# A transformer block on one core: the conditioning vector taken up ahead of the other parameters, and two GpSimd operations of the second norm moved to VectorE

## The reference, cut to what matters

```python
mod_x = jax.nn.silu(c) @ lp['ada_w'] + lp['ada_b']
mod_c = jax.nn.silu(c_ctx) @ lp['ada_w'] + lp['ada_b']
shx1, scx1, gx1, shx2, scx2, gx2 = [t[:, None, :] for t in jnp.split(mod_x, 6, axis=-1)]
hx = modulate(rms_norm(x, lp['norm_pre_mix']), shx1, scx1)
hc = modulate(rms_norm(ctx, lp['norm_pre_mix']), shc1, scc1)
...
x = x + gx1 * rms_norm(merge_branches(px[..., MIX_IN:], yx_a, yx_b, lp), lp['norm_post_mix'])
hx = modulate(rms_norm(x, lp['norm_pre_ffn']), shx2, scx2)
x = x + gx2 * rms_norm(swiglu(hx, lp), lp['norm_post_ffn'])
```

## Time and profile before

| | us |
|---|---|
| median of 3 runs | 2158.22 |
| lowest and highest run | 2155.16, 2163.36 |
| the profiled execution, its own time | 2160.06 |
| its span in the trace | 2158.2 |
| TensorE busy | 2024.2 |
| VectorE busy | 1252.0 |
| ScalarE busy | 808.1 |
| GpSimd busy | 269.8 |

### The profile page before, as it was taken

The page is one execution under the profiler, slowest core; times in us unless marked ns, Lnnn a source line. Parts: engine busy times, 40 slices in busy tenths (PEclk is TensorE's granted clock), DMA queues, the critical chain, the costliest instruction groups (busy, mean ns, idle before and its releaser), DMA issues. The chain is left out here.

```text
span 2158.2 us, 35947 instructions
## 1 busy us (share of the span) xinstructions
PE 2024.2 (94%) x15475; PEld 1655.1 (77%) x15475; DVE 1252.0 (58%) x1160; ACT 808.1 (37%) x895; POOL 269.8 (12%) x132
## 2 busy tenths in 40 slices
PE   5899999999999989977899899989999999999998
PEld 3367888888788876656788688878888888888886
DVE  2365666665556347768878487564445455444445
ACT  2232121212263235435544465533334333433333
POOL 0023121312304034301000020120000000000000
PEclk9899999999999999989999999999999999999999
DMA  8988888887555389978442578626556555555553
GB/s 301 382 288 310 314 313 320 290 319 269 153 147 131 88 230 313 283 164 194 97 91 58 93 233 321 215 78 195 185 184 194 188 185 191 194 204 192 192 193 116
DMA packets 355505, 453.62 MB, mean 210 GB/s; under 512 B 106062, under 2 KB 261054, under 8 KB 338094
## 3 DMA queue, kind: packets, MB, share of 16 engines
q1 hardware_dynamic: 347760, 440.59, 64.4%
q10 hardware_dynamic: 7614, 11.10, 1.4%
HBM read 413.43 MB, written 38.22 MB: 209 GB/s over the span
## 5 line engine op out<-in xcount | busy, mean ns | idle before, releaser
L221 DVE TENSOR_TENSOR f_w_lo<-t_w_raw,f_w_hi 128x2048 fp32r<-128x2048 f32 x130 | 297.9, 2292 | 363.5 <-ACT f_w_hi L214 363.5
L214 ACT ACTIVATE f_w_hi<-t_w_raw 128x2048 fp32r<-128x2048 f32 x132 | 252.7, 1916 | 436.7 <-PE pf L2963 288.6
L2961 PE MATMUL pf<-f_w_hi,h 128*128 128x512 f32 x688 | 268.5, 390 | 0.0
L2963 PE MATMUL pf<-f_w_hi,h 128*128 128x512 f32 x688 | 267.7, 389 | 0.0
L2962 PE MATMUL pf<-f_w_lo,h 128*128 128x512 f32 x688 | 267.7, 389 | 0.0
L214 ACT ACTIVATE p_w_hi<-h_w_raw 128x2048 fp32r<-128x2048 f32 x48 | 89.2, 1909 | 334.0 <-DVE stage L761 252.2
L906 DVE SCALAR_TENSOR_TENSOR late_acc<-h_of_x,siluc,late_acc 128x2048 f32<-128x2048 f32 x60 | 162.7, 2712 | 44.7 <-DMA h_of_x<-in_ada_w 43.1
L3009 PE MATMUL d_out<-f_w_hi,hid 128*128 128x512 f32 x704 | 176.4, 390 | 0.3 <-DVE f_w_lo L221 0.3
L266 PE MATMUL p_in<-h,p_w_lo 128*128 128x512 f32 x448 | 174.3, 389 | 0.0
L265 PE MATMUL p_in<-h,p_w_hi 128*128 128x512 f32 x448 | 174.3, 389 | 0.0
L264 PE MATMUL p_in<-h,p_w_hi 128*128 128x512 f32 x448 | 174.3, 389 | 0.0
(11 more groups left out here) (429 smaller groups left out, 3470.3 us busy)
## 6 DMA issues: line engine op xcount, KB each, us to landing
h_of_x<-in_ada_w SPq DMA_DIRECT2D x64, 1024.0 KB, 5.2
h_w_raw<-in_w_in SPq DMA_DIRECT2D x48, 1024.0 KB, 7.6
t_w_raw<-in_ffn_w_gate SPq DMA_DIRECT2D x44, 1024.0 KB, 5.2
t_w_raw<-in_ffn_w_up SPq DMA_DIRECT2D x44, 1024.0 KB, 5.2
t_w_raw<-in_ffn_w_down SPq DMA_DIRECT2D x44, 1024.0 KB, 4.9
h_w_raw<-in_ada_w SPq DMA_DIRECT2D x32, 1024.0 KB, 10.5
gate_w<-in_w_in SPq DMA_DIRECT2D x30, 1024.0 KB, 6.0
t_w_raw<-in_w_out SPq DMA_DIRECT2D x16, 1024.0 KB, 5.8
```

The costliest lines, as they stand in the source:

```text
L214: act.activation(self.hi[:, m % self.S, 0:w] if to is None else to, self.raw[:, s, 0:w], ACT.Copy)\
L221: eng.tensor_tensor(lo, self.raw[:, s, 0:w], b32(hi), ALU.subtract)\
L2961: pe.matmul(o, h[:, 0], hi[:, at], start=k == 0, stop=False)
L2963: return pe.matmul(o, h[:, 1], hi[:, at], start=False, stop=k == KT - 1)
```

## The change

In the first stage, `c` and `c_ctx` are the only rows that ScalarE loads. The other 22 transfers go to SyncE behind the fourth modulation tile. TensorE transposes c by itself, VectorE copies it to a tile of its own (`ccol`), ScalarE's sigmoid stands between the first and the second square, and the two silu operations stand ahead of the statistics on VectorE. The products of the first modulation tile come ahead of the first pair of turns, one pair now follows each of the first eight tiles, and the three transposes of the parameters stand behind the fourth pair. At the second norm, the low part of weight tile 3 and the copy of the first half's h leave GpSimd; VectorE makes the low part directly behind the second diagonal, and the copy behind the last low part of h.

```diff
-                for tile, row, n, w, src in pieces:
-                    act.dma_start(prow[row:row + n, tile, 0:w], src).then_inc(s_prow, 16)
-                for n in range(4):
+                for tile, row, n, w, src in c_pieces:
+                    act.dma_start(prow[row:row + n, tile, 0:w], src).then_inc(s_crow, 16)
...
+                token_square(0)
+                act.wait_ge(s_ccol, 1)
+                act.activation(sigc[:], ccol[:], ACT.Sigmoid).then_inc(s_sig, 1)
+                for n in range(1, 4):
+                    token_square(n)
...
+                    if t == RAW - 1:
+                        sp.wait_ge(s_const, 1)
+                        for tile, row, n, w, piece in other_pieces:
+                            sp.dma_start(prow[row:row + n, tile, 0:w], piece).then_inc(s_prow, 16)
...
-                    if t < 7:
-                        for b in range(2 + 2 * t, 4 + 2 * t):
+                    if t == 0:
+                        pe.wait_ge(s_diag, 4)
+                    if t < 8:
+                        for b in range(2 * t, 2 * t + 2):
                             turn(b)
+                    if t == 3:
+                        pe.wait_ge(s_const, 10)
+                        pe.wait_ge(s_prow, 16 * len(other_pieces))
...
-                pool.wait_ge(fring.lo_odd, 1)
-                fring.split_lo(pool, 3, 3, to=[t[:] for t in apart[3]])
-                pool.wait_ge(s_hlo0, 4)
-                pool.wait_ge(s_o, 8)
-                pool.tensor_copy(h2[:, :, :, 0:P].rearrange("p a k t -> p (a k) t"),
-                                 b32(h0).rearrange("p a k t -> p (a k) t")).then_inc(s_h0, 1)
...
                 unit_rows(1)
+                dve.wait_ge(fring.lo_odd, 1)
+                fring.split_lo(dve, 3, 3, to=[t[:] for t in apart[3]])
                 for g in range(4):
                     h_of(1, g)
                     if g:
                         h_lo(g - 1)
                 h_lo(3)
+                dve.wait_ge(s_o, 8)
+                dve.tensor_copy(h2[:, :, :, 0:P].rearrange("p a k t -> p (a k) t"),
+                                b32(h0).rearrange("p a k t -> p (a k) t")).then_inc(s_h0, 1)
```

More of the change, by code:

```diff
@@ L335, in phase_inputs @@
     s_const = sem("i_constants_made")
+    s_crow, s_cT, s_ccol = (sem(f"i_c_{n}") for n in ("rows_landed", "transposed", "columns_copied"))
     s_prow = sem("i_param_rows_landed")
@@ L376, in phase_inputs @@
         sigc = alloc(st, "sigc", [P, 2 * KT])
+        ccol = alloc(st, "c_columns", [P, 2 * KT])
+        C_ROW = COL["c"] % P
+        c_rows = prow[C_ROW:C_ROW + 2 * KT, COL["c"] // P, :]
+        c_pieces = [p for p in pieces if p[0] == COL["c"] // P and C_ROW <= p[1] < C_ROW + 2 * KT]
+        other_pieces = [p for p in pieces if not (p[0] == COL["c"] // P and C_ROW <= p[1] < C_ROW + 2 * KT)]
         sel = alloc(st, "sel", [P, 2])
@@ L485, in columns @@
                     last.then_inc(s_modp, 1)
[L486 to L494, removed]
+                pe.wait_ge(s_crow, 16 * len(c_pieces))
+                pe.transpose(p_col[:, 0:2 * KT], c_rows, ident[C_ROW:C_ROW + 2 * KT, C_ROW:C_ROW + 2 * KT]).then_inc(s_cT, 1)
                 pe.wait_ge(s_sc, 1)
@@ L502, in _ @@
                     last.then_inc(s_used, 1)
-                    if t < 7:
-                        for b in range(2 + 2 * t, 4 + 2 * t):
+                    if t == 0:
+                        pe.wait_ge(s_diag, 4)
+                    if t < 8:
+                        for b in range(2 * t, 2 * t + 2):
                             turn(b)
+                    if t == 3:
+                        pe.wait_ge(s_const, 10)
+                        pe.wait_ge(s_prow, 16 * len(other_pieces))
+                        for r in range(PROWS):
+                            last = pe.transpose(p_col[:, r * P:(r + 1) * P], prow[:, r, :], ident[:])
+                        last.then_inc(s_prmT, 1)
                     if q == 1 and p:
@@ L517, in _, with token_square @@
                 act.wait_ge(s_const, 1)
[L518 to L520 removed]
+                for tile, row, n, w, src in c_pieces:
+                    act.dma_start(prow[row:row + n, tile, 0:w], src).then_inc(s_crow, 16)
+                def token_square(n):
                     act.wait_ge(s_xt[n], 16)
@@ L562, in _ @@
                     dve.tensor_scalar(diag[:, n, :], ident[:], stat[:, 1, n:n + 1], None, ALU.mult).then_inc(s_diag, 1)
+                for b in range(8):
+                    evac(b)
+                dve.wait_ge(s_prmT, 1)
+                dve.tensor_copy(prm[:], p_col[:, 0:PROWS * P]).then_inc(s_prm, 1)
                 dve.wait_ge(s_prm, 1)
[L564 to L571 removed]
                 mu = prm[:, COL["mu"]:COL["mu"] + 29]
@@ L613, in _ @@
                 row(0)
-                for b in range(10, 14):
+                for b in range(8, 12):
                     evac(b)
@@ L618, in _ @@
                     if j == 0:
-                        evac(14)
-                        evac(15)
+                        for b in range(12, 16):
+                            evac(b)
                     row(2 * j + 1)
```

17 lines of the change are left out of this document (8 added, 9 removed).

## The result

The changed kernel took 2146.08 us (median of 7 runs, 2141.4 to 2148.42) beside 2160.73 us for the kernel before (7 runs): a ratio of 0.9921, with a 95% interval of 0.9905 to 0.9937. (The ratio on record is not the quotient of the two medians, which is 0.9932 and lies in the same interval.) The forecast was 2145.3, in a range of 2141 to 2150. A second comparison gave 2146.1 beside 2161.74 and again 0.9921 (0.9900 to 0.9942). The time came out 0.8 us from the forecast, and part of that is luck. The forecast had a gain of 12.9 us, a ratio of 0.9940, which lies just outside the first interval and at the edge of the second. The measured gain is larger: some 17 us by the ratio (13.6 to 20.5), 14.7 by the medians. The times agree this closely because the seven runs of the kernel before have a median 2.5 us above the 2158.22 that the forecast started from.

The account below looks back on a forecast made before the run. TensorE, busy 94% of the span, was taken as the bound; the norm's 9.1 us plus the first stage's 3.8 (4.2 - 0.9 + 0.5) gave 12.9, from 2158.22 to 2145.3 us, range 2141 to 2150.

Parts of the forecast that it names:

- The norm, 9.1 us: Second norm: without GpSimd's two operations beside VectorE's additions, TensorE saves 7.0 us of idle time and 2.1 of slow clock.
- The copy: Second norm: VectorE's copy of 128x4096 takes at most 4.6 us, hidden at cost 0 with 0.7 us slack.
- Rival (e): Second norm: VectorE's copy is far dearer than a subtraction and makes the kernel slower, 2166.8 us; 2%.
- The low part of tile 3: Second norm: on VectorE directly behind the diagonal, 2.29 us, hidden with 1.6 us to spare.
- The fourth square: First stage, ScalarE: starts at 14.2 instead of 18.38, with turns 4.68 us behind it, 4.2 us earlier.
- The clock of the first pair: First stage, TensorE: working on the first tile just before shortens the slow part by 0 to 1.7 us, taken as 0.5.
- The transposes: First stage, TensorE: three parameter transposes now stand between turns instead of inside the wait, costing 0.9 us.
- (d): First stage: c lands late, at 16.9, so only 5.3 us are gained, 2152.9 us; 3%.
- SyncE's 22 issues: First stage: the parameter transfers moved to SyncE end by 12 to 19 us, hidden.
- Handed on to the stage's end: First stage: its 3.8 us gain reaches the stage's end, because the transfers behind 48.44 are the same and start earlier.
- Rival (a): First stage: its gain is lost before the stage ends, with a second half-clock stretch costing 3.6 us; 2148.9 us; 15%.
- Rival (b): First stage: the half-clock stretch near its end goes, adding 3.6 us for 16.5 in all, 2141.7 us; 8%.

Follow-up runs that it names:

- e12: The changed kernel without any further change, traced a third time and timed again; traced span 2146.4 us.
- e1: Against the kernel before, only the first stage's part of the change, GpSimd keeping its two operations at the norm; 2153.08 us, ratio 0.9968.
- e10: Against the changed kernel, TensorE turns the first two token tiles ahead of the first modulation product again; traced span 2147.4 us.
- e8: Against the changed kernel, the 22 other parameter transfers are issued by ScalarE again, right behind c; traced span 2145.8 us.

## Why the prediction was right, and where it was not

- **The norm, 9.1 us:** 6.97 of idle time (t0 to t1: 21.81 to 14.84, the same in every trace that has this part) and 2.09 of clock, 9.06. The additions were priced at 1.18 + 3 x 0.7 = 3.3 and took 3.17. Only the instruction beside the first was misnamed: it is the product for h, no low part.
- **The copy:** taken at its upper bound of 4.6, measured 2.28. The step that failed is the row that stood for it: 4096 columns of the copy take as long as 2048 of the subtraction. And the reading that the trace has no copy of VectorE from SBUF to SBUF was wrong. It has several, these two among them (count, busy us, mean ns):

```profile
L1486 DVE COPY first_b<-ident 64x512 f32<-64x512 f32 x2 | 0.8, 418 | 0.0
L1487 DVE CAST eye_r<-ident 128x128 fp32r<-128x128 f32 x1 | 0.2, 227 | 0.0
```

  By these two rows a further column costs 0.5 ns, and 4096 columns some 2.2 us, an estimate that would have been right to 0.1. The Trainium skill, "VectorE: DVE Perf Modes", section "Mode 2×_2P — use both read ports for one tensor", says that an operation with one SBUF tensor can make two results per cycle, in float32 too, and one with two tensors can't. By that the price is halved as well, and the 2.28 us of both agree. The copy's cost was 0 either way, and the slack at this place is more than was given. Rival (e) had no ground.
- **The low part of tile 3:** 2.28, directly behind the diagonal, hidden, as said.
- **The fourth square** started at 13.29 and not 14.2: the landing of the last tokens was taken from before (11.9 us after issue), and it came 0.9 sooner. The 4.68 behind it held to 0.01 us (17.98). But two things end there at once: the diagonals are ready at 17.93 and the first product ends at 17.98, so diagonals that were ready still earlier would have gained nothing.
- **The clock of the first pair:** taken as 0.5, between 0 and 1.7. It was 0.8 in the first trace, and 0 to 1.0 in the others.
- **The transposes:** priced 0.87, from a row at the slow start; they cost 0.43 (0.49 long) where they stand now. 5.08 - 0.43 + 0.80 = 5.45, near the 5.56 by which SyncE is earlier, where I had 3.8. That c lands well inside the tokens' traffic was right (4.7 and 5.1 us after issue), and (d) fell.
- **SyncE's 22 issues** were to end by 19 and ended at 22.97, because its four tile issues took 9.26 us where I had let them end near 5. So its next load went out at 23.02, 5 us after the first product (16.10 + 1.94) had freed the slot. TensorE did not wait for that tile: it works without a break up to the sixteenth turn.
- **Handed on to the stage's end:** with the stretch at its late place, of 5.27 us at SyncE 4.92 arrived (e12), 4.65 of 5.14 (e1), 2.04 of 2.28 (e10), all against the first trace of the kernel before. Against its second trace, with the shorter stretch, e12 has 4.1 of 5.9. So most of the gain is handed on, but how much of it is known only to about 1 us. Rival (a) fell in the form that I gave it.
- **The term that was mis-sized** is then the first stage: 3.8 forecast, 4.9 with the late stretch, 8.1 without. Rival (b), with 8%, was true of two of the three traces of the changed kernel, and of two of the nine with the new order and ScalarE free, with 3.2 us instead of 3.6; I had taken the stretch as fixed to its place, though the earlier trace rows showed that it follows a wait for a transfer, and the change moves the transfers. With the norm's 9.06 that makes 14 to 17 us, which lies within the ratio's interval (13.6 to 20.5).

## What to carry to other kernels

Look at what an engine has to issue before its first useful instruction: 22 small transfers on ScalarE held up everything behind its squares, and moving them to a queue that had time for them cost nothing that these traces show. A GpSimd instruction that reads SBUF should not stand beside VectorE's two-input instructions on a critical chain, for each takes on the length of what it meets. And before a difference of a few us between two traces is explained, trace the same kernel twice: the places at which TensorE's clock falls moved by themselves here and were worth 3 us each.

## What the runs showed of the hardware

- An issue is not always short: four issues of 1 MB tiles behind four others kept SyncE for 9.26 us (22 issues on ScalarE in e8: 0.3 to 0.5 each), though each tile had its own free buffer. Small transfers behind them in the same queue wait for that.
- Products at the start run at half speed with the granted clock read as 1.00: eight of 128x512 took 1.94 us at 16.10 and 1.06 at 20.82 in the changed kernel. It lasts into the first turns, by 0.6 to 1.7 us.
- Beside a GpSimd memset the additions of VectorE keep their 0.74 us, beside its copy of the same size they take on its length.
